# Seven half-size products for the first input projection, with gates kept in DRAM and a long convolution summed in PSUM

## The reference, cut to what matters

```
h = rmsnorm(x, g_mix)
z = h @ w_in                       # 1024 -> 4608 columns: 36 tiles of 128
a_val, a_gt, sc_b, sc_c, sc_v      # 5 x 512 columns; then 2 x 1024 gate columns
g_a, g_b = sigmoid(gates + b_gate)
a = causal_dwconv(a_val * sigmoid(a_gt), conv_a_w) + conv_a_b        # 31 taps, 4 tiles
a = silu(layernorm(a));  y_a = a @ w_a_out                           # 512 -> 1024
s = sc_b * causal_dwconv(sc_c * sc_v, conv_b_w);  y_b = s @ w_b_out  # 3 taps
x = x + (g_a * y_a + g_b * y_b) @ w_o
```

## Time and profile before

| | us |
|---|---|
| median of 3 runs | 1992.83 (1992.31 to 1997.02) |
| span of the profiled execution | 1992.7 |
| TensorE matmuls busy | 1955.2 (98%) |
| VectorE busy | 1307.8 (66%) |
| POOL busy | 840.8 (42%) |
| ScalarE busy | 580.7 (29%) |

### The profile page before, as it was taken

One profiled execution on the slowest core, in us unless ns is written; L12 is line 12 of the kernel. 1 busy time (PEld: TensorE's weight loads), 2 busy tenths in 40 slices (PEclk: granted clock), 3 DMA queues, 4 the chain that ended last, 5 costly groups with the idle time before them and its releaser, 6 DMA issues.

```text
span 1992.7 us, 24952 instructions
## 1 busy us (share of the span) xinstructions
PE 1955.2 (98%) x9341; PEld 1624.8 (82%) x9341; DVE 1307.8 (66%) x1294; ACT 580.7 (29%) x755; POOL 840.8 (42%) x597
## 2 busy tenths in 40 slices
PE   7999999999999999999999999999999999999998
PEld 6888888888788888888887788878787878888887
DVE  5989997311547988889888785665723845666621
ACT  4001002300325333333341200243312245565511
POOL 2444454455323565555666555323133512212321
PEclk9999999999999999999999999999999999999999
DMA  4111111142111322322236434111132210000043
GB/s 153 53 42 53 37 47 48 40 116 71 53 43 43 95 85 74 95 69 89 93 136 232 133 124 169 54 32 42 32 115 65 81 41 1 11 12 1 1 138 95
DMA packets 188606, 145.28 MB, mean 73 GB/s; under 512 B 10019, under 2 KB 171760, under 8 KB 188528
## 3 DMA queue, kind: packets, MB, share of 16 engines
q1 hardware_dynamic: 187248, 141.84, 23.0%
q10 hardware_dynamic: 1280, 2.35, 0.3%
HBM read 124.25 MB, written 19.92 MB: 72 GB/s over the span
## 4 chain that ended last, share of the span: by engine, by line
PE 83%; DVE 8%; issue 4%; ACT 2%; POOL 2%; DMA 1%; ACTq 0%; POOLq 0%; DVEq 0%; SPq 0%
PE ps L647 51%; PE ps L872 19%; PE ps L1105 2%; PE ps L1138 1%; PE ps L1140 1%; PE ps L1139 1%; POOL wlo L561 1%; PE ps L1116 1%; PE ps L1119 1%; PE ps L1122 1%; PE ps L1113 1%; PE ps L1125 1%; DVE win_a L2280 1%; PE ps L714 1%; DVE prob L2328 1%
## 5 line engine op out<-in xcount | busy, mean ns | idle before, releaser
L556 POOL TENSOR_TENSOR small<-ones 128x1 f32<-128x1 f32 x124 | 43.1, 348 | 751.7 <-PE ps L647 676.0
L561 POOL TENSOR_TENSOR wlo<-raw,whi 128x1024 fp32r<-128x1024 f32 (+1 forms) x121 | 338.1, 2794 | 10.1
L647 PE MATMUL ps<-xa_hi,whi 128*128 128x512 f32 x992 | 312.6, 394 | 3.3 <-DVE xa_lo L1928 0.9
L647 PE MATMUL ps<-xa_lo,whi 128*128 128x512 f32 x992 | 308.3, 389 | 0.0
L647 PE MATMUL ps<-xa_hi,wlo 128*128 128x512 f32 x992 | 308.2, 389 | 0.0
L647 PE MATMUL ps<-xb_hi,whi 128*128 128x512 f32 x768 | 241.6, 394 | 6.6 <-DVE xb_lo L2236 1.9
L647 PE MATMUL ps<-xb_lo,whi 128*128 128x512 f32 x768 | 238.6, 390 | 0.0
L647 PE MATMUL ps<-xb_hi,wlo 128*128 128x512 f32 x768 | 238.3, 390 | 0.0
L647 PEld LDWEIGHTS ps<-xa_hi,whi 128*128 128x128 f32 x992 | 184.0, 188 | 44.6 <-issue 2.4
L647 PEld LDWEIGHTS ps<-xa_hi,wlo 128*128 128x128 f32 x992 | 186.2, 188 | 39.2
L647 PEld LDWEIGHTS ps<-xa_lo,whi 128*128 128x128 f32 x992 | 186.2, 188 | 38.9
(11 more groups left out here) (373 smaller groups left out, 3427.3 us busy)
## 6 DMA issues: line engine op xcount, KB each, us to landing
raw<-in_w_in SPq DMA_DIRECT2D x52, 512.0 KB, 3.8
t<-in_w_mod SPq DMA_DIRECT2D x48, 256.0 KB, 2.8
f_scratch<-t SPq DMA_DIRECT2D x22, 512.0 KB, 2.7
raw<-in_w_down SPq DMA_DIRECT2D x22, 512.0 KB, 4.0
raw<-in_w_up SPq DMA_DIRECT2D x40, 256.0 KB, 3.7
w_raw<-in_w_up SPq DMA_DIRECT2D x40, 256.0 KB, 3.8
f_raw_a<-f_scratch SPq DMA_DIRECT2D x5, 1024.0 KB, 5.7
x_columns<-in_x SPq DMA_DIRECT2D x8, 512.0 KB, 4.8
```

The source lines that it names most:

```text
L556: nc.gpsimd.tensor_tensor(small[:, 106 + slab.slot:107 + slab.slot], ones[:, 0:1], ones[:, 0:1], ALU.mult)
L561: nc.gpsimd.tensor_tensor(lo, src, f32(hi), ALU.subtract).then_inc(split_done, 1)
L647: ins = mm(dst[j], w, r[j], start=first and f, stop=last and l)
```

## The change

Of the 18 pairs of projection tiles, the first GLU pair stays as it is. The other 17 pairs (3 GLU, 6 of the short branch, 8 of gates) are computed one after another as seven products of half size. A pair is two output tiles; its weight matrix (1024 x 256) and h (1024 x 1024) are cut in quarters. Product k is 4 input tiles x 3 = 12 matmuls of 512 tokens, 84 a pair instead of 96. Products 1, 6, 7 and 4 add up in one PSUM bank, which is read in between; 2 has a bank, and 5 and 3 share one. Three banks serve a pair and the three others the next. Product 1 of the next pair comes before products 4 and 3 of this one.

- Start: POOL forms h = hi + lo for tokens 0 to 639, ScalarE copies it from PSUM for the other three groups; VectorE makes four differences of quarters of h (`token_sub`), ScalarE and VectorE split them into `XBh` and `XBl`.
- Per pair: SP loads four quarters of weights (256 KB each); VectorE makes three weight sums (`win_sums`) and POOL the fourth (`win_third_sum`); ScalarE rounds the source of each product (`win_hi`), POOL makes its low part (a ring of four); ScalarE copies PSUM three times (`win_copy`), VectorE adds three times (`win_c11`, `win_c22`, `win_c12`).
- The gates are now computed right after the short branch, all eight pairs of them, before either branch's output matmuls. Their sigmoids are stored to DRAM (`gdram`) and loaded again one by one through a ring of four buffers. The result of the short branch is stored to DRAM as well (`sdram`) and comes back in two loads of 1 MB.
- The long convolution adds up in banks 6 and 7 of PSUM (`conv_ps`); only the last tap of a tile writes SBUF. 5 to 10 taps lie in each pair from the second on.
- Then eight jobs `mix_b` and eight `mix_a` of 24 matmuls each follow, with weight slabs that hold two jobs each. The layernorm lies under `mix_b`.
- Loops over pairs and jobs are written out. SBUF buffers move; semaphore names are used again further on with an offset.

TensorE's list for a product and for a pair:

```diff
+        def win_product(p, k):
+            g = WIN_AT[p, k]
+            slot, cols = win_ring(g)
+            o = win_bank(p, k)
+            pe.wait_ge(sem("win_split"), g + 1)
+            if p == 0 and k in (6, 5, 7, 4):
+                pe.wait_ge(sem("tok_dve"), {6: 5, 5: 6, 7: 7, 4: 8}[k])
...
+            if k in (6, 7, 4):
+                pe.wait_ge(sem("win_copy"), 3 * p + {6: 1, 7: 2, 4: 3}[k])
+            if k == 3:
+                pe.wait_ge(sem("win_add"), 3 * p + 2)
...
+        win_product(0, 1)
+        for p in range(NWP):
+            for k in (2, 6, 5, 7):
+                win_product(p, k)
+            if p + 1 < NWP:
+                win_product(p + 1, 1)
+            for k in (4, 3):
+                win_product(p, k)
```

The tap, and VectorE's list for a pair and behind the last one:

```diff
+                if k == 0:
+                    ts(conv_ps, source, col("conv_a_w", i), col("conv_a_b", i), ALU.mult, ALU.add).then_inc(sem("conv_tap"), 1)
+                else:
+                    stt(conv_ps if k < TAPS_A - 1 else conv[:, i, :], source, col("conv_a_w", i + 4 * k), conv_ps,
+                        ALU.mult, ALU.add).then_inc(sem("conv_tap"), 1)
...
+            win_c11(p)
+            taps_of(a, b)
+            win_c22(p)
+            win_sums(p + 1, (1,))
+            taps_of(b, c)
+            win_c12(p)
+            win_sums(p + 1, (4,))
...
+            if p == NWP - 1:
+                for c in range(2):
+                    k0, c0 = S_PLACE[c]
+                    dve.wait_ge(sem("tok_hi"), 5 + c)
+                    tt(XBl[:, k0:k0 + 4, c0:c0 + H], hraw[:, k0:k0 + 4, c0:c0 + H], f32(XBh[:, k0:k0 + 4, c0:c0 + H]),
+                       ALU.subtract).then_inc(sem("tok_dve"), 1)
```

SP's queue in the branches:

```diff
+        def gate_load(r):
+            if r >= 4:
+                sp.wait_ge(sem("mix_done"), r - 3)
+            sp.dma_start(gate_ring(r)[:, 0:S], gdram[(8 + r) % 16]).then_inc(*gate_in(r)[:1], 16)
...
+        for q in range(1, 4):
+            if q >= 2:
+                slabk(Lin(SLABS["mix_b"] + q), A["w_b_out"][0], KC, q * 2 * P, 2 * P)
+            gate_load(2 * q + 2)
+            gate_load(2 * q + 3)
+        for q in range(4):
+            slabk(Lin(SLABS["mix_a"] + q), A["w_a_out"][0], KC, q * 2 * P, 2 * P)
+            if q < 3:
+                gate_load(2 * q + 10)
+                gate_load(2 * q + 11)
+            if q == 0:
                 sp.wait_ge(job_done, JOBS["mix_a"])
...
+            for m in (2 * q, 2 * q + 1):
+                c0 = H if m >= 4 else 0
+                for u, to in enumerate((xcolh, hraw)):
+                    sp.dma_start(to[:, m, c0:c0 + H].rearrange("p (t f) -> p t f", f=P),
+                                 A["x"][0, u * H:(u + 1) * H, m * P:(m + 1) * P].rearrange("(t p) f -> p t f", p=P)
+                                 ).then_inc(sem(f"load_in{m // 4}"), 16)
```

More of the change, by code:

```diff
@@ L367, in sync_program, with win_load @@
[L367 to L370, removed]
[L371 to L378 removed]
+        def win_load(p):
+            first, second = win_columns(p)
+            for r in range(4):
+                c = (first, second)[r // 2]
+                sp.dma_start(win_raw(p, r).rearrange("p (k n) -> p k n", n=P),
+                             w_in[H * (r % 2):H * (r % 2 + 1), c:c + P].rearrange("(k p) n -> p k n", p=P)
+                             ).then_inc(sem(f"win_raw{p % 2}"), 16)
@@ new lines, in tensor_program @@
+        first_bank_free(pe, NWP - 2)
+        pe.wait_ge(sem("win_add"), 3 * NWP - 3)
+        for m in range(KD):
+            J, L = Lin(JOBS["mix_b"] + m), Lin(SLABS["mix_b"] + m // 2)
+            pe.wait_ge(*((pair_free[J.slot], J.half())))
+            if m % 2 == 0:
+                pe.wait_ge(split_done, L.val(1))
+            if m == 1:
+                pe.wait_ge(sem("win_add"), 3 * NWP)
+            branch_product(J, L, m, S_PLACE, m % 2 == 0, ("s",) if m == 0 else None)
+            if m == 1:
+                pe.wait_ge(sem("ln_v"), 3)
+                first_bank_free(pe, NWP - 1)
+                for a in (0, H):
+                    last = mm(PS[:, ST + a:ST + a + H], ones[:, :], T[1][:, a:a + H], start=True, stop=True)
+                last.then_inc(sem("ln_pe"), 1)
+            if m == 4:
+                column_sums(T[1], 8, 0, sem("ln_v"), 10)
+            if m == 5:
+                broadcast(T[2][:, 0:1024].rearrange("p (t n) -> p t n", n=P), 8, 1)
@@ L1360, in scalar_program @@
-        act.wait_ge(*free(Lin(JOBS["short"] - 1)))
-        with act.Fori(0, 2) as q:
-            for u in range(2):
-                J = Lin(JOBS["short"] + 3 * u, 6, q)
-                act.wait_ge(job_done, J.val(1))
-                fn(T[0][:, 0:S], pair(J), ACT.Copy).then_inc(*one(free(J)))
-                act.wait_ge(*free(J + 1))
-                fn(T[2][:, 0:S], T[1][:, 0:S], ACT.Copy, scale=dcol("conv_b_w", q * 2 + u)).then_inc(sem("cv_ready"), 1)
-                act.wait_ge(sem("s_ready"), q * 2 + (u + 1))
-                fn(tile(XBh, q * 2 + (4 + u)), T[3][:, 0:S], ACT.Copy).then_inc(sem("branch_hi"), 1)
@@ new lines, in pair_products, with short_taps @@
+        def pair_products(p, first, second, into):
+            dve.wait_ge(sem("win_add"), 3 * p + 3)
+            tt(into[0], win_bank(p, 4), first, ALU.mult).then_inc(sem("pair_dve"), 1)
+            tt(into[1], pd[p % 2][:, H:S], second, ALU.mult).then_inc(sem("pair_dve"), 1)
+        def short_taps(i):
+            for k in range(1, TAPS_B):
+                if k == 1:
+                    dve.wait_ge(sem("pair_act"), pair_act(3 + 3 * (i // 2) + i % 2, 1))
+                else:
+                    dve.wait_ge(sem("short_tap"), 2 * i + k - 1)
+                stt(T[2 + i % 2][:, 0:S], T[1][:, k:k + S], col("conv_b_w", i + 4 * k), T[2 + i % 2][:, 0:S],
+                    ALU.mult, ALU.add).then_inc(sem("short_tap"), 1)
@@ new lines, in vector_program @@
+        dve.wait_ge(sem("h_raw"), 5)
+        dve.wait_ge(sem("x_hi"), 8)
+        for n in range(4):
+            token_sub(n)
+        win_sums(0, (1,))
+        token_low2(0, 3)
+        token_low2(1, 3)
+        J = Lin(JOBS["glu"])
+        dve.wait_ge(*free(J))
+        dve.wait_ge(job_done, J.val(2))
+        tt(gpad[:, 0, LPAD:LPAD + S], pair(J + 1), T[0][:, 0:S], ALU.mult).then_inc(sem("pair_dve"), 1)
+        after_all(*one(free(J + 1)))
+        win_sums(0, (4,))
+        token_low2(2, 3)
```

667 lines of the change are left out of this document (458 added, 209 removed).

## The result

The changed kernel takes 1981.59 us in the median of four runs (1980.39 to 1983.69); the kernel before, run beside it, takes 1994.92 (1992.31 to 1997.63). The ratio is 0.9936, 95% interval 0.9922 to 0.995: some 13 us or 0.6% faster. The forecast was 1974.4, a gain of 18.3 us. The profiled executions have spans of 1978.6 and 1992.7, 14.1 apart. The changed kernel's profiled execution took 1980.39, so 1.8 us lie around a span, and the executions of the kernel before show the same 1.8 (1992.15 us with a span of 1990.3); I had put it at nothing and so started from 1992.7 where some 1994.5 would have been right. Of the 7.2 us by which the forecast is too low, 1.8 are this, 4.2 the difference between 18.3 and 14.1, and 1.2 the distance from the profiled execution to the median.

A forecast was written before the change was run, and what follows sets the result against it. The prediction took TensorE's number of matmuls as the bound between first GLU pair and output projection. Removing 48.5 us, less returning waits and clock loss, gave -18.3 from 1992.7: 1974.4 us, range 1955 to 1992.

The forecast's parts named there:

- likeliest case: The prediction's own forecast of 1974.4 us, with its own range of 1966 to 1984; chance 51%.
- work removed: TensorE between first GLU pair and output projection: 464.8 us before, 416.3 us of work after, so -48.5 us.
- start: After the first GLU pair: queued roundings and low parts make TensorE wait, 4.3 us of it at product 1; +4.6 us.
- pairs: The seventeen half-size pairs: VectorE nearly full with taps at 1.32 us; priced 0 to 12, taken as +2 us.
- to the branches: From products to branch job 0: the short branch's low part queues behind VectorE's last add; +3.6 us.
- b branch: First eight branch jobs: bank wait 0.5, late weights before job 4 3.9, layernorm low parts 2.0; +6.4 us.
- a branch: Last eight branch jobs: weights late behind gates and x columns, 5.9 before job 2, 4.6 before job 6; +10.5 us.
- clock: TensorE's clock halves for some 3 us behind waits, each costing half its length, four counted; +4 us (0 to 8).
- behind it: Output projection: its low parts are now early, so TensorE's former wait goes; -0.9 us.
- Rival 3: Long convolution: the PSUM tap is no cheaper than the old mean of 1.705, +34.7 us, 2009 us; chance 8%.
- M plus bytes plus split: Late a-branch weights: from mixing time M, 8.6 us for loads, then POOL's split of 3.75 to 4.65; ready at M + 12.8.
- Rival 1: Branch weight loads are not late: 14.4 us of the branches and half the clock loss go, 1958 us; chance 22%.

The follow-up runs named there:

- Warm waits: Idle matmuls put ahead of five waits of TensorE in the changed kernel; 1974.31 us, ratio 0.9905 to the kernel before.
- sum in SBUF: Changed kernel with the running sum of the long convolution back in SBUF; 2030.52 us, ratio 1.0175 to the kernel before.
- slabs first: Changed kernel with each branch weight slab ahead of gate loads and x columns in SP's queue; 1964.79 us, ratio 0.9851 to the kernel before.
- slabs first with the earlier layernorm: Changed kernel with weight slabs first in SP's queue and the layernorm's column sums and broadcast one branch job earlier; 1959.36 us, ratio 0.9828.
- x columns behind: Changed kernel with only the a branch's x-column loads (1 MB) moved behind the next weight slab; 1971.21 us, ratio 0.9868 to the kernel before.
- start's order: Changed kernel with ScalarE rounding the first two products' weights ahead of h's combinations and VectorE's first GLU product earlier; 1981.07 us, ratio 0.9939.
- hand-over: Changed kernel with the low part of the first half of s ahead of the last pair's last add; 1978.73 us, ratio 0.9922.
- combined: Changed kernel with slabs first, start's order, hand-over and the layernorm one job earlier, all together; 1954.15 us, ratio 0.9808 to the kernel before.
- combined warm: The combined kernel plus three idle matmuls before product 6 and two before branch job 0; 1955.61 us, ratio 0.9811.
- PSUM alone: Kernel before the change, with the long convolution's running sum kept in PSUM within each run of taps; 1991.74 against 1993.77 us, ratio 0.9988.

## Why the prediction was right, and where its sizes were off

The sign, the mechanism and the places of the waits were right, and the time lies in the range, in the likeliest case's own too (1966 to 1984). By one of its own signs the sum was off: the output projection begins at 500.56 and not near 494. By its steps, in us of the profiled executions:

| step | predicted | trace | |
|---|---|---|---|
| work removed | -48.5 | -48.5 | 19.04 a pair and the matmuls as counted, 46.3; the other 2.2 are the gaps of the kernel before |
| start | +4.6 | +6.2 | 0.5, 4.0, and 1.65 before product 6 |
| pairs | +2 | +0.8 | one wait of 0.78, in pair 16 |
| to the branches | +3.6 | +3.1 | |
| b branch | +6.4 | +3.8 | 0.38 + 2.96 + 0.41 for 0.5 + 3.9 + 2.0 |
| a branch | +10.5 | +12.15 | 6.84 + 0 + 5.31 for 5.9 + 0 + 4.6 |
| clock | +4 | +9.0 | 1.7 + 1.35 + 1.6 + 1.75 + 2.6 |
| small gaps | 0 | +1.9 | what is left of the stretch to 500.56 |
| behind it | -0.9 | -2.5 | |
| sum | -18.3 | -14.1 | |

- **The clock is the term that was mis-sized**: it was put at 4 us and cost 9.0. The whole error is 4.2; the other terms nearly cancel. I took four stretches of 3 us. There are five, of 3.4, 3.4, 3.4, 6.8 and 6.8 us, 5.8 us of which lie inside the waits; half of the rest, 18 us, is 9.0. Warm waits gave 7.3 back in the medians (5.7 up to the output projection in its trace), where 9.0 less the 1.7 hidden at the start would be 7.3.
- **The gaps** were put at nothing without a reason. The prediction found 2.2 us of them among the matmuls before, let them go, and took them off with the work: 464.8 less 416.3 is 48.5, the matmuls alone are 46.3. The changed kernel has 1.9 us of the kind again. So the sum promised about 2 us that did not come. What makes these gaps was not tried.
- **The start.** The wait of the first product came as worked out (4.02 for 4.3). What I missed is a step of the changed list: ScalarE's first copy writes where the sigmoid of the first GLU tile lies, so it waits for VectorE's GLU product, which stands behind two low parts of 3.34 us each. It came at 60.14, and so product 6, not product 1, is the one that counts. I had also let VectorE's steps there be mostly uncontended; the four differences, 10.25 us, were near the 9.9 that I summed, but the first two low parts took 3.34 each where I used 2.3 to 2.8.
- **The pairs** have the cadence of the earlier trace rows and no wait but one. The tap, priced at 1.32 between 1.27 and 1.705, is 1.287. Rival 3 had the right mechanism and too low a price: its condition (the tap no cheaper) was made in sum in SBUF and cost 48.9, not 34.7, since the tap is 1.947 then.
- **The branches.** The order in SP's queue, "M plus bytes plus split", holds in its parts: 9.2 us from the last gate's issue to POOL's start for 8.6 predicted, 5.5 for the split where 3.75 to 4.65 was the range. The layernorm's 2.0 looked overrated with 0.4, but was hidden: slabs first brought 3.7 to light.
- **Rival 1** (loads not late) is false for the changed kernel, but its price, 1958, is near what slabs first with the earlier layernorm reaches by making it true: 1959.36.
- **Behind the output projection's start**, 0.3 comes from the shorter wait for `xa_lo` (0.6 for 0.9 in the earlier trace rows) and 1.7 from the drop in the earlier trace rows, which this execution of the changed kernel does not have: its clock reads 1.00 in all windows from 1288 to 1302, behind the same dip (1.41 of 2 us busy from 1290 to 1292). The drop is there again in six traces with the changed kernel's products (slabs first with and without the earlier layernorm, x columns behind, warm waits, start's order, hand-over) and missing in combined, combined warm and sum in SBUF, and in PSUM alone. So this part of the 14.1 is most likely no property of the change. The other 0.5 us stay open. It fits that executions of one kernel lie some us apart with the mean clock (the handover kernel 0.993 at 1975.06, 0.990 at 1980.97); which drop each of them had was not recorded.

## What to carry to other kernels

When work is taken from the bound engine, go through every queue that feeds the next stage with the new, shorter distances: here loads that nobody needed yet stood ahead of late weights, and an order that cost nothing to change was worth 16.8 us, over a third of the 46.3 that the removed matmuls are worth. Price a wait of TensorE with the clock behind it (here 15 us of waits at the late slabs carried 6 more), and expect the wait that a longer one hid. A part that does nothing alone, the sum in PSUM with 0.1%, can be what makes the rest possible: ask what the engine beside it will do once it is busier.

## What the runs showed of the hardware

- TensorE's granted clock fell from 2.4 to 1.2 GHz at the end of or just behind waits of 4.0, 3.1, 3.0, 6.8 and 5.3 us in the changed kernel, for 3.4 us each at the three short ones and 6.8 at the two long ones (3.5 of the 6.8 at the longest wait lie inside it). Waits of the same length did not always do the same: behind the 4.0 at the start it was 6.8 us in x columns behind, hand-over and slabs first with the earlier layernorm; at job 4 of the b branch there was none behind 3.15 in hand-over and 3.04 in start's order, and 6.8 at 2.92 in x columns behind; behind 3.3 before product 6 there was 3.4 in combined and start's order and none in warm waits. Behind waits of 2.1 and 1.5 none was seen. The Trainium skill ("TensorE: Matmul & The Clock Gate", Part 1) says that what watches the engine's activity runs free of the program, so that the same kernel comes out differently from run to run. These rows fit that, though each is of another kernel; the two groups of x columns behind, 0.996 and 0.992 of one kernel, agree with it directly.
- VectorE's tap and POOL's subtraction lengthen each other: 1.29 to 1.95 and 1.34 to 2.00 us in the mean, in the pairs when the tap reads both inputs from SBUF. Of more than 200 taps that read their sum from PSUM, in two kernels, the longest took 1291 ns.
- One MB more in front of a load on SP's queue delayed it by 4.0 us (262 GB/s), against 310 GB/s in the earlier trace rows.
